# Gathering the selected pages of a decode step: 128 indirect DMAs of GpSimd replaced by 224 plain DMAs of SyncE whose block numbers come from registers

## What is computed

```python
_, idx = lax.top_k(imp, min(N_SELECT, n_sel))            # 16 blocks of 64 tokens, per sequence and KV head
kb = k_sel.reshape(B, n_sel, SEL_BLOCK, G, D).transpose(0, 3, 1, 2, 4)
vb = v_sel.reshape(B, n_sel, SEL_BLOCK, G, D).transpose(0, 3, 1, 2, 4)
kg = kb[bi, gi, idx].reshape(B, Tq, G, n_keys, D)
vg = vb[bi, gi, idx].reshape(B, Tq, G, n_keys, D)
s2 = jnp.einsum('btgrd,btgsd->btgrs', q, kg)
p_sel = masked_softmax(s2, kpos <= qpos)
o_sel = jnp.einsum('btgrs,btgsd->btgrd', p_sel, vg)
```

## Time and profile before

| What | Value |
|---|---|
| Time, median of 3 runs | 1089.61 us (1089.56 to 1090.8) |
| Profiled execution, time | 1090.35 us |
| Profiled execution, span | 1088.5 us |
| PE, DVE, ACT, POOL busy | 835.6, 449.5, 190.0, 140.9 us |
| Data moved by DMA | 222.07 MB, mean 204 GB/s |
| Mean granted TensorE clock | 0.843 of full |

### The profile page before, as it was taken

One profiled execution on the slowest core, in us unless ns is written; L12 is line 12 of the kernel. 1 busy time (PEld: TensorE's weight loads), 2 busy tenths in 40 slices (PEclk: granted clock), 3 DMA queues, 4 the chain that ended last, 5 costly groups with the idle time before them and its releaser, 6 DMA issues.

```text
span 1088.5 us, 14190 instructions
## 1 busy us (share of the span) xinstructions
PE 835.6 (77%) x4877; PEld 412.7 (38%) x4877; DVE 449.5 (41%) x972; ACT 190.0 (17%) x484; POOL 140.9 (13%) x166
## 2 busy tenths in 40 slices
PE   6979967969687899999993036887113899877898
PEld 3555432434334344453661122334001343534443
DVE  2212306242042368765300017870003876558552
ACT  2101100010020021221310002430001433224200
POOL 0000000000000001000156730005673000000000
PEclk9989989889897899999975556997555998886899
DMA  9966569597875978878051126962224877484001
GB/s 343 317 200 233 184 204 340 182 286 270 274 225 188 343 255 315 307 257 273 24 185 49 53 80 212 365 211 82 86 90 158 293 278 268 146 314 189 1 39 40
DMA packets 122017, 222.07 MB, mean 204 GB/s; under 512 B 15945, under 2 KB 48882, under 8 KB 120474
## 3 DMA queue, kind: packets, MB, share of 16 engines
q1 hardware_dynamic: 115514, 203.79, 54.4%
q0 software_dynamic: 6432, 17.38, 4.8%
HBM read 215.25 MB, written 10.04 MB: 207 GB/s over the span
## 4 chain that ended last, share of the span: by engine, by line
PE 59%; DVE 11%; issue 9%; SPq 9%; another core or an unknown queue 8%; DMA 4%; ACT 1%; DVEq 0%; ACTq 0%
PE banks L560 13%; PE banks L538 12%; SPq L387 7%; PE banks L968 5%; PE banks L773 4%; PE banks L574 3%; DVE att L1620 3%; PE banks L506 3%; PE banks L825 2%; PE banks L841 2%; DMA proj<-in_cmp_cache 1%; PE banks L915 1%; SPq L382 1%; PE banks L519 1%
## 5 line engine op out<-in xcount | busy, mean ns | idle before, releaser
L560 PE MATMUL banks<-ring,xt 128*128 128x512 f32 x448 | 199.7, 599 | 0.0
L538 PE MATMUL banks<-proj,wide 128*64 128x256 f32 x896 | 111.5, 415 | 45.1 <-DMA proj<-in_cmp_cache 45.1
L1834 POOL DMA_INDIRECT ring<-in_sel_cache,index x128 | 121.1, 946 | 147.1 <-PE banks L915 99.1
L560 PEld LDWEIGHTS banks<-ring,xt 128*128 128x128 f32 x448 | 83.8, 192 | 106.0 <-issue 105.9
L841 PE MATMUL banks<-consts,wide 128*128 128x128 f32 x240 | 47.1, 325 | 89.5 <-issue 51.6
L1185 ACT ACTIVATE wide<-banks,att 128x128 f32<-128x128 f32 (+3 forms) x128 | 66.4, 523 | 217.0 <-DVE att L1620 173.8
L538 PEld LDWEIGHTS banks<-proj,wide 128*64 128x64 f32 x896 | 68.9, 151 | 89.3 <-DMA proj<-in_cmp_cache 49.7
L773 PE MATMUL banks<-ring,small 128*32 128x512 f32 x512 | 89.5, 735 | 6.5 <-DMA ring<-in_dv_cache 4.0
L1351 DVE TENSOR_SCALAR small<-small 128x510 f32<-128x510 f32 x8 | 3.4, 426 | 194.1 <-ACT small L1037 177.2
L1619 DVE TENSOR_TENSOR banks<-banks,consts 128x256 f32<-128x256 f32 x64 | 27.4, 428 | 124.0 <-remote 78.7
L841 PEld LDWEIGHTS banks<-consts,wide 128*128 128x128 f32 x240 | 31.1, 164 | 119.7 <-issue 64.7
(11 more groups left out here) (336 smaller groups left out, 904.3 us busy)
## 6 DMA issues: line engine op xcount, KB each, us to landing
ring<-in_dk_cache SPq DMA_DIRECT2D x256, 256.0 KB
ring<-in_dv_cache SPq DMA_DIRECT2D x256, 256.0 KB
proj<-in_cmp_cache SPq DMA_DIRECT2D x224, 128.0 KB, 2.8
ring<-in_w_in SPq DMA_DIRECT2D x7, 2048.0 KB, 10.7
ring<-in_x_nat SPq DMA_DIRECT2D x2, 2048.0 KB
ring<-in_cmp_cache SPq DMA_DIRECT2D x32, 128.0 KB, 4.2
ring<-in_w_out SPq DMA_DIRECT2D x1, 4096.0 KB, 12.2
out_s_win<-in_win_nat SPq DMA_DIRECT2D x1, 4088.0 KB
```

The source lines that it names most:

```text
L538: last = mm(to, w1[:, kv, half, lp, :], rows[:, kv, g, lp, :, :, :], start=lp + half == 0, stop=lp == LP - 1 and half == 1, tile_position= ...
L560: last = mm(banks[:, 3 + n % 2, :], xt[:, k, P * t:P * t + P], w_ring[:, c % 2, k, :], start=k == 0, stop=k == KC - 1)
L1834: nc.gpsimd.indirect_dma_start(out=sel_kv[:, q, m, :], out_offset=None, in_=src["sel_cache"][:, :], in_offset=bass.IndirectOffsetOnAxis(ap ...
```

## The change

The selection cache is laid out the same way in memory, but declared as blocks of [64 x 128]. What DVE hands over is now a list of block numbers in one row (`ids`, 13 for each of the 16 pairs) and not 128 row numbers per slot. SP reads the numbers into registers and issues one plain DMA per ranked block (32 KB, `sel_ranked`) and two per sequence for the fixed blocks (64 KB, both KV heads at once, `sel_fixed`): 8 + 104 = 112 per half, 224 in all.

- First half: at v = 4 SP waits for the last projection tile, then issues the 8 fixed DMAs; at each of v = 4 to 11 it issues the 13 ranked blocks of one pair (three register loads, of 4, 4 and 5 numbers) ahead of the four V pages.
- Second half: at v = 29 SP waits for `sel_out` of the first half and issues 8 fixed DMAs; at each of v = 29 to 54 it issues 4 ranked blocks, each with a register load of its own, ahead of the four V pages.

GpSimd's 128 indirect DMAs are gone; its 8 small DMAs for the new tokens' V rows stay and now wait for `sel_cleared`. DVE clears the upper half of the last slot with a MEMSET before each half. On DVE two arithmetic instructions on [128 x 128] become two copies of one row; on PE two matmuls become one.

```diff
@@ in program
+        def sel_ranked(eng, kind, q, first, last):
+            _, blocks = nc.values_load_multi_w_load_instructions(
+                ids[0:1, bass.ds(N_TOP * q + first - SEL_FIRST, last - first)], engines=[kind], min_val=0, max_val=N_POOL * 4 - 1,
+                skip_runtime_bounds_check_because="the DMA checks its own address")
+            for n, at in zip(range(first, last), blocks):
+                eng.dma_start(sel_kv[64 * (n % 2):64 * (n % 2) + 64, q % 8, n // 2, :],
+                              src["sel_cache"][bass.ds(at, 1), :, :].rearrange("o k n -> (o k) n")).then_inc(s("sel_in"), 16)
+
+        def sel_fixed(eng, kind, b):
+            halves = src["sel_cache"][:, :, :].rearrange("(a h g) k n -> a h k g n", h=2, g=2)
+            for t in range(2):
+                _, (at,) = nc.values_load_multi_w_load_instructions(
+                    pages[0:1, bass.ds(b * PAGES + (PAGES - 1) * t, 1)], engines=[kind], min_val=0, max_val=N_POOL - 1,
+                    skip_runtime_bounds_check_because="the DMA checks its own address")
+                eng.dma_start(sel_kv[64 * t:64 * t + 64, 2 * (b % 4):2 * (b % 4) + 2, 0, :],
+                              halves[bass.ds(at, 1), t, :, :, :].rearrange("o k g n -> (o k) g n")).then_inc(s("sel_in"), 16)
@@ SyncE, the V part
+            def sel_load(q):
+                sel_ranked(sp, mybir.EngineType.SP, q, SEL_FIRST, 6)
+                sel_ranked(sp, mybir.EngineType.SP, q, 6, 10)
+                sel_ranked(sp, mybir.EngineType.SP, q, 10, SEL_LAST)
             for v in range(64):
+                if v == 4:
+                    sp.wait_ge(s("proj_ready"), 32)
+                    sp.wait_ge(s("new_proj_ready"), NCHUNK)
+                    sp.wait_ge(s("index_ready"), 1)
+                    for b in range(4):
+                        sel_fixed(sp, mybir.EngineType.SP, b)
+                if 4 <= v < 12:
+                    sel_load(v - 4)
+                if v == 29:
+                    sp.wait_ge(s("sel_tensor"), sel_step(0, "sel_out"))
+                    for b in range(4, DEC):
+                        sel_fixed(sp, mybir.EngineType.SP, b)
+                if 29 <= v < 55:
+                    q, slot = 8 + (v - 29) // 13 * 4, SEL_FIRST + (v - 29) % 13
+                    for n in range(4):
+                        sel_ranked(sp, mybir.EngineType.SP, q + n, slot, slot + 1)
                 if v == 60:
...
                 load_v(v)
@@ TensorE
-                    for par in range(2):
-                        last = mm(banks[64 * par:64 * par + 64, 2, 0:P], ones[:, :], spread[:, P * par:P * par + P],
-                                  start=True, stop=True, tile_position=(0, 64 * par))
-                    last.then_inc(s("index_spread"), 1)
+                    mm(banks[0:1, 2, 0:2 * P], ones[:, 0:1], spread[:, :], start=True, stop=True).then_inc(s("index_spread"), 1)
@@ VectorE
-            L(V.tensor_scalar(spread[:, 0:P], banks[:, 2, 0:P], 64.0, None, ALU.mult))
-            V.tensor_scalar(index[:, :], spread[:, 0:P], const("iota64"), None, ALU.add).then_inc(s("index_ready"), 1)
+            V.tensor_copy(to[:, :, 0:N_TOP:2], turned_ids[:, 0, :, 1:SP_SLOTS])
+            V.tensor_copy(to[:, :, 1:N_TOP:2], turned_ids[:, 1, :, 1:SP_SLOTS - 1]).then_inc(s("index_ready"), 1)
+            def sel_clear():
+                V.memset(sel_kv[64:128, :, SP_SLOTS - 1, :], 0.0).then_inc(s("sel_cleared"), 1)
@@ GpSimd
-            pool.wait_ge(s("index_ready"), 1)
             for n in range(2):
-                if n:
-                    pool.wait_ge(s("sel_tensor"), sel_step(0, "sel_out"))
-                for q in range(8):
-                    for m in range(SP_SLOTS):
-                        col = (8 * n + q) * SP_SLOTS + m
-                        nc.gpsimd.indirect_dma_start(
-                            out=sel_kv[:, q, m, :], out_offset=None, in_=src["sel_cache"][:, :],
-                            in_offset=bass.IndirectOffsetOnAxis(ap=index[:, col:col + 1], axis=0)).then_inc(s("sel_in"), 16)
-
-                pool.wait_ge(s("sel_in"), 16 * 64 * (n + 1))
+                pool.wait_ge(s("sel_cleared"), n + 1)
```

More of the change, by code:

```diff
@@ L90, in const_table @@
     parts["diag"] = parts["diag"].reshape(P, 32)
-    parts["iota64"] = (row % 64)[:, None]
     of, bg = row // 16, row % 16
@@ L158, in laid_out @@
         "cmp_cache": f(cmp_kv.transpose(0, 3, 6, 4, 5, 2, 1).reshape(n_pool, P, 256)),
-        "sel_cache": f(sel.reshape(n_pool * 2 * NKV * 64, P)),
+        "sel_cache": f(sel.reshape(n_pool * 2 * NKV, 64, P)),
         "dk_cache": f(dk.transpose(0, 3, 2, 1).reshape(n_pool, P, 512)),
@@ L193, in program @@
         k_new = sb("k_new", [P, 6, DEC])
-        index = sb("index", [P, P], I32)
+        ids = sb("ids", [1, 16 * N_TOP], I32)
         sample = sb("sample", [DEC, COLS])
@@ L199, in program @@
         pages_bg = sb("pages_bg", [P, 11], I32)
-        ones = sb("ones", [P, 64])
+        ones = sb("ones", [P, 1])
         work = sb("work", [P, 160])
-        picked = sb("picked", [P, 112])
+        picked = sb("picked", [P, 96])
         proj = sb("proj", [P, TILES, COLS])
@@ L254, in program @@
         chosen = xn[:, 1600:1600 + 8 * N_TOP].rearrange("p (s j) -> p s j", j=8)
-        p_kc_t, block_row = picked[:, 0:32], picked[:, 96:107]
+        p_kc_t, block_row = picked[:, 0:32], small[:, 4:15]
         p_hid = picked[:, 32:96].rearrange("p (k n) -> p k n", k=2)
@@ L374, in sel_step @@
             return n * next(len(at) for at in STEPS.values() if name in at) + step(name)
+        def sel_ranked(eng, kind, q, first, last):
[13 more added lines that the diff above has]
+                              halves[bass.ds(at, 1), t, :, :, :].rearrange("o k g n -> (o k) g n")).then_inc(s("sel_in"), 16)
+        SEL_FIRST, SEL_LAST = 2, 2 + N_TOP
+        SEL_DMAS = 4 * 2 + 8 * N_TOP
         block = ctx.enter_context(nc.Block())
@@ L1512, in _ @@
             dve.wait_ge(s("index_spread"), 1)
-            L(V.tensor_scalar(spread[:, 0:P], banks[:, 2, 0:P], 64.0, None, ALU.mult))
-            V.tensor_scalar(index[:, :], spread[:, 0:P], const("iota64"), None, ALU.add).then_inc(s("index_ready"), 1)
+            turned_ids = banks[0:1, 2, 0:2 * P].rearrange("p (t q m) -> p t q m", t=2, q=16)
+            to = ids[:, :].rearrange("p (q n) -> p q n", q=16)
+            V.tensor_copy(to[:, :, 0:N_TOP:2], turned_ids[:, 0, :, 1:SP_SLOTS])
+            V.tensor_copy(to[:, :, 1:N_TOP:2], turned_ids[:, 1, :, 1:SP_SLOTS - 1]).then_inc(s("index_ready"), 1)
             sum_new(6)
@@ L1667, in keep_v @@
                 V.tensor_copy(o_diff[:, :, b], banks[:, 7, 0:4]).then_inc(s("o_diff_kept"), 1)
+            def sel_clear():
+                V.memset(sel_kv[64:128, :, SP_SLOTS - 1, :], 0.0).then_inc(s("sel_cleared"), 1)
             def sel_place(n):
-                dve.wait_ge(s("sel_in"), 16 * 64 * (n + 1))
+                dve.wait_ge(s("sel_in"), 16 * SEL_DMAS * (n + 1))
+                dve.wait_ge(s("sel_cleared"), n + 1)
                 for g in range(2):
@@ L1709, in sel_keep_out @@
                               ).then_inc(s("sel_vector"), 1)
+            dve.wait_ge(s("proj_ready"), 32)
+            dve.wait_ge(s("new_proj_ready"), NCHUNK)
+            sel_clear()
             for j in range(DUOS + 4):
@@ L1738, in _ @@
                         sel_keep_out(n)
+                        if n == 0:
+                            sel_clear()
             dve.wait_ge(s("new_out_turned"), 1)
```

## The result

| Quantity | Before | Forecast | Measured after |
|---|---|---|---|
| Time, median | 1089.7 us | 1046 (1025 to 1074) | 1099.3 us (1099.04 to 1099.53, 4 runs) |
| Ratio to before | 1 | 0.96 | 1.0086 [1.0068, 1.0103] |
| V step 11 runs at | 678.7 | 643.5 | 672.8 |
| First half's scores (L885, now L925) at | 706.9 | | 707.2 |
| `sel_out` at | 741.4 | 706 | 741.6 |

The change made the kernel 0.9% slower. That is small, but the interval leaves out 1. The parts of the span give the difference of the spans, 1097.6 - 1088.5 = 9.1 us: 0.2 to `sel_out`, 2.6 in the second half, 6.3 behind it. Against the forecast (unrounded, 706.4 and 161.3 in the table) they are 53 us: 35.2, 14.6 and 3.3.

A forecast was written before the change was run, and what follows sets the result against it. The prediction took two holes, where POOL's gathers hold up the other engines, to bound 85 and 90 us. It summed 1090.35 - 35 (first half) - 12 (second half) + 3 (clock) = 1046.4, stated as 1046 us, range 1025 to 1074.

The forecast's parts named there:

- 161.3: Second half, from `sel_out` to its scores: forecast time in us, 173.3 before, with SP's issue setting the pace.
- The price of one ranked block, 0.333 us: SP's stream, both halves: issue time of one 64-row DMA, taken from the median of 512 DMAs of 128 rows.
- The register loads: SP's stream: each load was put at 0.326 us, three for the 13 ranked blocks of a first-half V step.
- forecast 89.5: First half: us of SP issue through V step 11's pages, 87.4 plus 2.5%.
- the 2.2 that the forecast had allowed: First half: 2.5% put on SP's issue sum of 87.4 us for small hitches.
- It goes on as before: First half from V step 12 on: PE would keep its earlier 4.2 us per step, with no added cost.
- 3 us for the clock: After the SP-paced stretch: PE partly at the lower clock, adding 3 us.
- SP's stream sets the pace of both stretches: V steps 4 to 11 come 10.3 us apart and second-half steps 5.9, limited by SP's issue.
- The holes were the gathers' doing: Two stretches of 85 and 90 us where PE is mostly idle while POOL gathers; each worth 70 us if won.
- SP itself is hit: Rival: late delivery or many small DMAs stretch SP's issue; 18% more ends the gain, 30% gives 1120 us; chance 0.08.
- PE at half clock: Rival: PE at 6.2 us per V step sets the second half's pace, 8 us more, 1055 us; chance 0.09.
- Cheap issue with fewer rows: Rival: a ranked DMA issues in half of 0.333 us, 35 us less, 1012 us; chance 0.06.

The follow-up runs named there:

- e1: Changed kernel with a tail after its last store in which SP issues six DMAs of each of twelve shapes, then register loads; 1303.0 us with the tail.
- e5: Changed kernel with each of the 208 ranked DMAs copying 32 rows instead of 64; 1066.1 us, 0.9762 of the kernel before.
- e2: Changed kernel with the first half's ranked numbers loaded four at a time from multiples of 16 bytes; 1084.5 us, 0.9935 of the kernel before.
- e11: e3 with the first half's 26 groups issued two ahead of each of V steps 4 to 16; 1060.6 us, 1.0982 of the kernel before.
- e3: e2 with one aligned load of four per V step in the second half too, in place of four single loads; 1062.6 us, 0.9724 of the kernel before.
- e6: Changed kernel with all 224 DMAs of selected blocks left out; 943.1 us, 0.8641 of the kernel before.
- e16: Kernel before with every second gather left out, 32 per half; 1003.8 us, 0.9190 of the kernel before.
- e17: Changed kernel with GpSimd fetching 64 plain 128-row DMAs per half, page numbers as addresses; 967.2 us, 0.8866 of the kernel before.
- e4: Changed kernel with the same 224 plain DMAs and loads issued by GpSimd, none by SP; 990.6 us, 0.9068 of the kernel before.
- e8_poolsplit: e7 with 8 of the 26 groups per half issued by SP instead of GpSimd; 955.8 and 955.7 us, 0.8736 and 0.8738 of the kernel before.
- e7: e4 with the ranked numbers loaded four at a time from multiples of 16 bytes; 960.5 us, 0.8781 of the kernel before.
- e12: Kernel before, unchanged, profiled again in set 4; 953.9 us in one run.

## Why the prediction was wrong

**The price of one ranked block, 0.333 us, was the step that failed.** It is 0.473 here and 0.468 in e1. I had bounded it by DMAs of 1, 8 and 128 rows (0.307 to 0.439), and 64 rows lie outside: between measured sizes I took the price to be monotonic. The DMAs of 1 and 8 rows also have fixed addresses, and e1 prices those otherwise (0.362 to 0.433 for 128 rows, in the place of 0.333), so they were no bounds for this form. 104 blocks are 14.6 us per half, 8 fixed blocks (0.598) 2.1; e5 gives 33 us back by this term alone.

**The register loads were priced by the nearest row, which was a special case.** A load of four V page numbers starts at a multiple of 16 bytes. The loads for 13 numbers per pair mostly don't: in six of eight V steps they take 0.87, 0.87 and 1.07 us in the place of 0.298, so 1.92 us each, 11.5 in all, and some 0.5 in the other two. The first half's stream, from its first register load (549.1) to the end of V step 11's issue (669.0), took 119.9 us, forecast 89.5. Of these 30.4 us, 14.6 + 2.1 + 12.0 = 28.7 are the three prices; 1.7 are hitches beyond the 2.2 that the forecast had allowed (in the trace 1.4 in the fixed blocks and 1.1 in the second pair's). V step 11 ran 29.3 us late, since SP began 2.5 us earlier than forecast and the last page landed 1.4 later. e2 took 12 us away. The second half's single loads are cheap; there the DMAs' 14.6 and 2.1 us, less 104 x 0.02 for loads of 0.278, make up 14.6 us, which is what was missing (175.9 against 161.3).

**The way back to speed was priced at nothing in the first half.** "It goes on as before" was wrong. From V step 11 to the first scores took 34.4 us, 28.2 before; PE had the same 181 matmuls (columns as in the earlier trace rows, the kernel before, then the changed one):

```profile
678.70:706.90 28.20, 25.32 (x181) 10.16 (x182) 23.25 (x69) 11.76 (x43) 0.00 (x0) 0.99 1.02 363
...
672.80:707.20 34.40, 32.74 (x181) 11.64 (x182) 22.05 (x62) 10.95 (x39) 0.00 (x0) 0.75 0.94 334
```

The forecast's own 3 us for the clock became 6.3 behind the second half, where L925 takes 7.52 us and took 5.16. Both of these follow stretches in which PE waited for SP. That the low clock costs these microseconds is read from the rows; no run changed the clock alone.

**What was right.** SP's stream sets the pace of both stretches (e5, e11). The holes were the gathers' doing, and go with them. The order of events was as forecast. With the right prices the sum comes close: 1046 + 31 for the DMAs (208 x 0.140 + 16 x 0.265, less 2 for the single loads) + 12 for the loads = 1089. The last 6 + 3 for the clock, to 1098, are read from this very result and test nothing. The second half's scores did wait for the last block, and PE's pace did not set that stretch. One reading was off without any effect: a V step of four 256 KB pages is 1.05 MB, and takes 2.9 us at 367 GB/s, not 2.7.

**The rivals.** "SP itself is hit" was nearest in time and gave the right breakeven: 119.9 + 173.9 = 294 us of stream are 19% over 247, and 18% was where the gain ended. Its mechanism, late delivery by traffic, was wrong in the main: the probe has the same price alone. "PE at half clock" had named 6.2 us per V step, and 6.2 is what came; that is chance, since in e3 the V steps came 5.4 us apart. "Cheap issue with fewer rows" is true for 32 rows (0.316), if far from half, and false for 64. By the Trainium skill, "DMA: Bandwidth & Descriptors", section "Issuing engines are not separate DMA queues", issue is usually small against the DMA. By that rule the time would have been 950; the trace disagrees more than I had said, with some 0.8 us of SP per block and its loads. The holes' disappearance was worth what I had said (e6: 943), and all of it went to SP.

The hole itself I called late delivery to all the engines while POOL gathers. That it depends on the indirect form is shown (e16 against e17, and e4); by what path a gather delays PE is not, and that it happens in some sets only was in no rival.

## What to carry to other kernels

Before small DMAs are put ahead of loads that an engine waits for, sum up the issuing stream with prices of exactly these shapes, register loads included; measure a shape that the trace lacks rather than interpolate. Load register values in fours from multiples of 16 bytes, and put plain DMAs with register addresses on an engine that nobody waits for: e8_poolsplit ran at 0.874 of the kernel before with holes, at 955.8 and 955.7 us in its two sets (against the level without holes, 961.5, it was not run side by side). The Trainium skill, "Perfetto Trace Analysis", section "DMA Optimizations", says that balancing DMAs across engines may help where descriptor generation is the bottleneck. Here moving all of them off SP gave 102 us (e7 against e3), and balancing them between GpSimd and SP (e8) 5 more, which is within the noise. A kernel with long trains of indirect DMAs may have a second level, here 14% slower; time it in several sets.

## What was unexpected of the hardware

- A DMA of SP whose address comes from a register takes 0.468 us with 64 rows and 0.333 with 128, at rows of 512, 1024 or 2048 bytes alike, and 0.315 with 32 or 16 rows of 512 bytes (e1, the shortest of each six). 64 rows of two pieces take 0.598.
- A register load in SP costs some 0.2 us for each further number (behind a wait mostly 435 to 445 ns for one, 1029 for four), but four numbers from a multiple of 16 bytes cost 0.30 us in the stream and 0.468 behind a wait. The Trainium skill, "Runtime: NRT & Kernel Launch", section "Instruction fetch mechanics", gives about 200 ns per register. The runs agree in the step from one number to the next, and disagree for four from a multiple.
- The kernel with 128 indirect DMAs took 1092.5 to 1092.8 us in three sets and 962.8 and 961.5 in two. The traces with a long time (the kernel before, e16) show the other engines held up, those with a short one (e12) do not. One chip gave both levels. The three kernels without gathers that ran in more than one set stayed within 0.2%.
